# Decay sums of the SSM mixer with constant triangles as one-pass weights

## The reference

```
dt  = softplus(dt_raw + dt_bias);  a = -exp(a_log)
acum = cumsum(dt * a) over the tokens of a chunk of 128
seg[t, s] = acum[t] - acum[s]                # sum of dt*a over s < r <= t
decay = exp(where(t >= s, seg, -inf))
w = (c . b) * decay * dt ;  y = w @ x        # per head
y += c . state * exp(acum)                   # second chunk sees the first through the state
...
blocks = concat(chunks[:-1], chunks[1:]) + pos_emb   # compressed keys and values
kc = silu(blocks @ w1) @ w2
```

## Time and profile before

| | us |
|---|---|
| median of 3 runs | 870.97 (870.74 to 872.29) |
| the profiled execution | 869.12 |
| its span in the trace | 867.3 |
| PE busy | 848.3 (98%) |
| DVE busy | 602.0 (69%) |
| ACT busy | 472.5 (54%) |
| POOL busy | 63.2 (7%) |

### The profile page before, as it was taken

The page is one execution under the profiler, slowest core; times in us unless marked ns, Lnnn a source line. Parts: engine busy times, 40 slices in busy tenths (PEclk is TensorE's granted clock), DMA queues, the critical chain, the costliest instruction groups (busy, mean ns, idle before and its releaser), DMA issues.

```text
span 867.3 us, 15125 instructions
## 1 busy us (share of the span) xinstructions
PE 848.3 (98%) x5994; PEld 777.9 (90%) x5994; DVE 602.0 (69%) x805; ACT 472.5 (54%) x680; POOL 63.2 (7%) x64
## 2 busy tenths in 40 slices
PE   6999999999999999999999999999999999999997
PEld 6999999999998999899999999888887888888885
DVE  5538986537877578687776777787664686666665
ACT  5457773348665444485564555556574554444442
POOL 0025920000000232000000000000000000000000
PEclk9999999999999999999999999999999999999999
DMA  9643452333433445564555455453324365444431
GB/s 349 221 152 135 158 195 97 104 141 113 169 122 122 167 157 202 202 207 172 195 179 205 155 188 195 146 182 125 132 97 171 121 219 216 182 184 185 183 139 48
DMA packets 22169, 143.83 MB, mean 166 GB/s; under 512 B 2929, under 2 KB 3189, under 8 KB 5729
## 3 DMA queue, kind: packets, MB, share of 16 engines
q1 hardware_dynamic: 20304, 138.30, 44.4%
q0 software_dynamic: 1808, 4.73, 1.6%
HBM read 141.96 MB, written 1.84 MB: 166 GB/s over the span
## 4 chain that ended last, share of the span: by engine, by line
PE 91%; DVE 3%; ACT 3%; issue 1%; DMA 1%; SPq 0%; DVEq 0%; ACTq 0%
PE pj L467 15%; PE pj L470 12%; PE pj L469 12%; PE pa L891 7%; PE pa L892 7%; PE pa L893 7%; PE pj L1106 5%; PE pj L472 2%; PE pj L471 2%; PE pj L1108 2%; PE pa L506 2%; PE po L1106 2%; PE pj L570 1%; ACT w_hi L1152 1%; PE pj L576 1%
## 5 line engine op out<-in xcount | busy, mean ns | idle before, releaser
L1638 DVE TENSOR_TENSOR w_lo<-w_raw,w_hi 128x2048 fp32r<-128x2048 f32 x127 | 293.3, 2319 | 49.3 <-ACT w_hi L1152 49.1
L467 PE MATMUL pj<-a_hl,w_hi 128*128 128x256 f32 x944 | 269.6, 286 | 0.3 <-issue 0.3
L469 PE MATMUL pj<-a_hl,w_hi 128*128 128x256 f32 x944 | 267.0, 283 | 0.0
L470 PE MATMUL pj<-a_hl,w_lo 128*128 128x256 f32 x944 | 267.0, 283 | 0.0
L1152 ACT ACTIVATE w_hi<-w_raw 128x2048 fp32r<-128x2048 f32 x127 | 242.1, 1908 | 40.5 <-PE pa L893 22.1
L467 PEld LDWEIGHTS pj<-a_hl,w_hi 128*128 128x128 f32 x944 | 181.0, 192 | 3.4 <-issue 2.9
L469 PEld LDWEIGHTS pj<-a_hl,w_hi 128*128 128x128 f32 x944 | 181.0, 192 | 0.3
L470 PEld LDWEIGHTS pj<-a_hl,w_lo 128*128 128x128 f32 x944 | 181.0, 192 | 0.0
L891 PE MATMUL pa<-w_hi,a_hl 128*128 128x512 f32 x280 | 109.4, 391 | 0.0
L892 PE MATMUL pa<-w_lo,a_hl 128*128 128x512 f32 x280 | 109.2, 390 | 0.0
L893 PE MATMUL pa<-w_hi,a_hl 128*128 128x512 f32 x280 | 108.9, 389 | 0.0
(11 more groups left out here) (273 smaller groups left out, 1218.2 us busy)
## 6 DMA issues: line engine op xcount, KB each, us to landing
w_raw<-stream SPq DMA_DIRECT2D x127, 1024.0 KB, 4.8
area<-gains POOLq DMA_DIRECT2D x4, 512.0 KB, 4.2
cst<-consts SPq DMA_DIRECT2D x1, 1093.0 KB, 13.3
x_tok<-x_in SPq DMA_DIRECT2D x2, 512.0 KB, 4.6
w_raw<-stream SPq DMA_DIRECT2D x4, 256.0 KB, 6.7
area<-cmpw POOLq DMA_DIRECT2D x1, 1024.0 KB, 6.0
out<-x_tok SPq DMA_DIRECT2D x4, 256.0 KB, 2.0
t_wide<-t_rows POOLq DMA_DIRECT2D x1, 768.0 KB, 10.8
```

The lines of the kernel that those rows point to most:

```text
L467: pe.matmul(out_, a[0], a[1], start=first, stop=False)
L469: pe.matmul(out_, wh, al, start=False, stop=False)
L470: return pe.matmul(out_, wl, ah, start=False, stop=last)
L1638: dve.tensor_tensor(w_lo[:, slot, :], w_raw[:, slot, :], w_hi[:, slot, :].bitcast(F32), ALU.subtract)\
```

## The change

1. `seg(g)` has the constants as stationary operand and the heads' values as moving one. The operands are fp32r: `ones` and `gt` are copied once into the free chunk 20 of `a_hi` (on POOL, at the start), and dt*a is kept as a pair, high part and rest, in `dta_hl`. `gate_decay(g)` now forms `le` times dt*a for 2 chunks of the sequence and 4 heads, once for the high part and once for the rest, into free chunks of `a_hi` and `a_lo` (8 to 11 for even groups, 12 to 15 for odd). Eight products of 512 columns take the place of the twelve float32 ones.
2. The layout of `E` is by kind of block, then head: S holds two blocks (1024 columns), T one (512), and `decay` and `ssm_w` follow.
3. `gate_decay(0)` moves from between the conv blocks to behind the masked scores `cb`.
4. The four `ckp` operations move from there to behind `ssm_w(3)`.
5. `dta` takes two operations instead of one, and two more make its pair.

```
--- before.py
+++ after.py
@@ -215,7 +215,7 @@
         xbc = V(36, 16, T)
         xc = [V(52, 2, T), V(54, 2, T)]
         xs_tok, xdt = V(0, 2, D), V(8, 2, D)
-        gdt, E = V(16, 2, 4, P), V(20, 4, 384)
+        E = V(20, 3, 4, P)
         cmp_w1 = V(26, 2, 16, 64)
         nq, cb = V(34, 4, T), V(38, 4, 384)
         kk, cm, vv = V(52, 2, T), V(54, 2, T), V(56, 2, T)
@@ -248,8 +248,10 @@
         rt, rcol, eps_t, warm = small(2), small(2), small(1), small(1)
         xsum, ysum, ybias, yrt, yr = small(2), small(4), small(2), small(2), small(2)
         dgr = sb("dgr", [P, 2, P])
+        dta_hl = sb("dta_hl", [P, 2, 4, 2, 4], F32R)
+        ones_gt_r = a_hi[:, 20, :]
         small40 = small(2, 40)
-        dtx, dt_, dta = small(2, 16), small(2, 16), small(2, 16)
+        dtx, dt_, dta = small(2, 16), small(2, 16), small(4, 2, 4)
         dt_e, ea = small(2, 16), small(16)
         gate = small(2, 24)
         ssy, ry = small(2, 4), small(2, 4)
@@ -318,6 +320,11 @@
 
             return po[:, 0:T] if n % 2 else pa[:, 3, 0:T]
 
+        def decays(g, part):
+
+            c = 8 + (g % 2) * 4
+            return (a_hi, a_lo)[part][:, c:c + 4, :]
+
         def await_value(eng, name):
 
             b, n = BANK[name]
@@ -384,6 +391,9 @@
         @block.gpsimd
         def _(gp):
             G = Order(gp, "pool_order")
+
+            gp.wait_ge(S("tri_loaded"), 16)
+            gp.tensor_copy(ones_gt_r, ones_gt).then_inc(S("tri_ready"), 1)
 
             def load_gain(j):
 
@@ -724,15 +734,19 @@
 
                 claim(pe, "S", f"seg{g}")
                 claim(pe, "T", f"seg{g}")
-                pe.wait_ge(S("gdt_ready"), g + 1)
-                for m in range(4):
-                    bank = (ps, pt)[m // 2][:, m % 2, :]
-                    pe.matmul(bank[:, 0:256], gdt[:, 0, m, :], le_ones, start=True, stop=True)
-                    pe.matmul(bank[:, 128:256], dta[:, 1, 4 * g + m:4 * g + m + 1].to_broadcast([P, P]), le,
-                              start=False, stop=True, skip_group_check=True)
-                    mm = pe.matmul(bank[:, 256:384], gdt[:, 1, m, :], le, start=True, stop=True)
-                    if m == 1:
-                        written(mm, "S")
+                pe.wait_ge(S("decays_ready"), 2 * g + 2)
+                pe.wait_ge(S("tri_ready"), 1)
+                ones_r, gt_r = ones_gt_r[:, 0:P], ones_gt_r[:, P:2 * P]
+                for part in range(2):
+                    pe.matmul(ps[:, 0, :], gt_r, decays(g, part)[:, 0:2, :], start=part == 0, stop=part == 1)
+                for part in range(2):
+                    pe.matmul(ps[:, 1, :], gt_r, dta_hl[:, part, g, 0, :].unsqueeze(2).to_broadcast([P, 4, P]),
+                              start=part == 0, stop=False)
+                for part in range(2):
+                    mm = pe.matmul(ps[:, 1, :], ones_r, decays(g, part)[:, 2:4, :], start=False, stop=part == 1)
+                written(mm, "S")
+                for part in range(2):
+                    mm = pe.matmul(pt[:, 0, :], gt_r, decays(g, part)[:, 2:4, :], start=part == 0, stop=part == 1)
                 written(mm, "T")
 
             def ssm_y(g):
@@ -742,10 +756,10 @@
                     pe.wait_ge(S("xdt_ready"), 2)
                 for m in range(4):
                     c = (4 * g + m) * 64
-                    pe.matmul(po[:, m * 64:(m + 1) * 64], E[:, m, 0:128], xdt[:, 0, c:c + 64], start=True, stop=True)
-                    pe.matmul(po[:, 256 + m * 64:256 + (m + 1) * 64], E[:, m, 128:256], xdt[:, 0, c:c + 64],
+                    pe.matmul(po[:, m * 64:(m + 1) * 64], E[:, 0, m, :], xdt[:, 0, c:c + 64], start=True, stop=True)
+                    pe.matmul(po[:, 256 + m * 64:256 + (m + 1) * 64], E[:, 1, m, :], xdt[:, 0, c:c + 64],
                               start=True, stop=False)
-                    mm = pe.matmul(po[:, 256 + m * 64:256 + (m + 1) * 64], E[:, m, 256:384], xdt[:, 1, c:c + 64],
+                    mm = pe.matmul(po[:, 256 + m * 64:256 + (m + 1) * 64], E[:, 2, m, :], xdt[:, 1, c:c + 64],
                                    start=False, stop=True)
                 written(mm, "O")
 
@@ -1337,9 +1351,10 @@
                                    ACT.Copy).then_inc(S("ck_ready"), 1)
 
             def decay(g):
-                for region, bank, m in (("S", ps, 0), ("T", pt, 2)):
-                    await_psum(act, region, f"seg{g}")
-                    read(act.activation(E[:, m:m + 2, :], bank[:, :, 0:384], ACT.Exp), region)
+                await_psum(act, "S", f"seg{g}")
+                read(act.activation(E[:, 0:2, :, :], ps.rearrange("p a (m t) -> p a m t", m=4), ACT.Exp), "S")
+                await_psum(act, "T", f"seg{g}")
+                read(act.activation(E[:, 2, :, :], pt[:, 0, :].rearrange("p (m t) -> p m t", m=4), ACT.Exp), "T")
 
             token_major(("vv", 0), vv)
             decay(0)
@@ -1841,9 +1856,11 @@
             tt(ws_lo, prm[:, o:o + 320], ws_hi.bitcast(F32), ALU.subtract).then_inc(S("ws_ready"), 1)
             def gate_decay(g):
 
-                tt(gdt, gt.unsqueeze(1).unsqueeze(1).to_broadcast([P, 2, 4, P]),
-                   dta[:, :, 4 * g:4 * g + 4].unsqueeze(3).to_broadcast([P, 2, 4, P]), ALU.mult)\
-                    .then_inc(S("gdt_ready"), 1)
+                for part in range(2):
+                    d = dta_hl[:, part, g, :, :].bitcast(F32).rearrange("p t (a m) -> p (t a) m", a=2)
+                    tt(decays(g, part).rearrange("p c (m t) -> p c m t", m=2),
+                       le.unsqueeze(1).unsqueeze(1).to_broadcast([P, 4, 2, P]),
+                       d.unsqueeze(3).to_broadcast([P, 4, 2, P]), ALU.mult).then_inc(S("decays_ready"), 1)
 
             narrow_out("dt", 40)
             conv_out(0)
@@ -1857,8 +1874,13 @@
             dve.wait_ge(S("ea_ready"), 1)
             V_.did(stt(dt_, dtx, 0.0, dt_e, ALU.max, ALU.add))
             V_.sync()
-            stt(dta, dt_, -1.0, ea.unsqueeze(1).to_broadcast([P, 2, 16]), ALU.mult, ALU.mult)\
-                .then_inc(S("dta_ready"), 1)
+            for tb in range(2):
+                V_.did(stt(dta[:, :, tb, :], dt_[:, tb, :].rearrange("p (g m) -> p g m", g=4), -1.0,
+                           ea.rearrange("p (g m) -> p g m", g=4), ALU.mult, ALU.mult))
+            V_.sync()
+            V_.did(dve.tensor_copy(dta_hl[:, 0], dta))
+            V_.sync()
+            V_.did(tt(dta_hl[:, 1], dta, dta_hl[:, 0].bitcast(F32), ALU.subtract))
             conv(1)
             conv_out(2)
             sb_sum(0)
@@ -1872,7 +1894,6 @@
             conv(5)
             sb_sum(1)
             conv_out(6)
-            gate_decay(0)
             conv_taps(6)
             conv_out(7)
             sb_mask(1)
@@ -1904,10 +1925,13 @@
 
                 await_read(dve, "T", "cb")
                 await_read(dve, "S", "cb")
-                for region, m in (("S", 0), ("T", 2)):
-                    await_read(dve, region, f"seg{g}")
-                    tt(E[:, m:m + 2, :], E[:, m:m + 2, :], cb[:, g, :].unsqueeze(1).to_broadcast([P, 2, 384]),
-                       ALU.mult).then_inc(S("ssm_w_ready"), 1)
+                await_read(dve, "S", f"seg{g}")
+                tt(E[:, 0:2, :, :], E[:, 0:2, :, :],
+                   cb[:, g, 0:256].rearrange("p (a t) -> p a t", a=2).unsqueeze(2).to_broadcast([P, 2, 4, P]),
+                   ALU.mult).then_inc(S("ssm_w_ready"), 1)
+                await_read(dve, "T", f"seg{g}")
+                tt(E[:, 2, :, :], E[:, 2, :, :], cb[:, g, 256:384].unsqueeze(1).to_broadcast([P, 4, P]),
+                   ALU.mult).then_inc(S("ssm_w_ready"), 1)
 
             def ssm_out(g):
 
@@ -1918,14 +1942,7 @@
                 V_.sync()
                 read(tt(y_tok[:, :, g * 256:(g + 1) * 256], two(po), xs_tok[:, :, g * 256:(g + 1) * 256], ALU.add), "O")
 
-            dve.wait_ge(S("ck_ready"), 4)
-            pos = prm_("pos").rearrange("p (v c) -> p v c", v=2)
-            for half in range(2):
-                for v in range(2):
-                    tt(ckp[:, half, v, :].rearrange("p (n c) -> p n c", c=8),
-                       ck[:, v, :, :].rearrange("p g t -> p (g t)").rearrange("p (n c) -> p n c", c=8),
-                       pos[:, v, half * 8:half * 8 + 8].unsqueeze(1).to_broadcast([P, 32, 8]), ALU.add)\
-                        .then_inc(S("ckp_ready"), 1)
+            gate_decay(0)
             ahead(("vv", 0))
             ssm_w(0)
             gate_decay(1)
@@ -1940,6 +1957,14 @@
             ahead(("z", 0))
             ssm_out(2)
             ssm_w(3)
+            dve.wait_ge(S("ck_ready"), 4)
+            pos = prm_("pos").rearrange("p (v c) -> p v c", v=2)
+            for half in range(2):
+                for v in range(2):
+                    tt(ckp[:, half, v, :].rearrange("p (n c) -> p n c", c=8),
+                       ck[:, v, :, :].rearrange("p g t -> p (g t)").rearrange("p (n c) -> p n c", c=8),
```

(2 more changed lines are left out.)

## The result

The changed kernel has a median of 863.61 us (861.35 to 864.36, 5 runs) against 870.89 (869.35 to 872.29, 5 runs): ratio 0.993, 95% interval 0.9911 to 0.9948. Two later comparisons, each with 11 runs of the kernel before beside it, gave 0.9932 (0.9915 to 0.9949) and 0.9933 (0.9919 to 0.9947). The profiled execution has 863.37 us after 869.12, 5.75 less. Predicted were 864.5 and a gain of 6.5.

The account below looks back on a forecast made before the run. PE was taken as the bound (busy 98% of the span). Products gain 6.74 us, less a 0.2 wait, is 6.5: 862.6 for the profiled execution, 864.5 for the median; 8-in-10 range 862.9 to 867.0.

Parts of the forecast that it names:

- What bounds: Whole kernel, window 127.4 to 182 us: PE sets the time, so microseconds taken from its program come off the end.
- The products: seg(0) to seg(3): eight one-pass products take 1.81 us; gain 1.70 in group 0, 1.68 in each other, together 6.74.
- Rivals B, C and D: Pace per seg product: B four passes, 0.86 us (chance 0.03); C stalled, 0.43 (0.04); D faster, 0.13 (0.02).
- The wait of group 0: Ahead of seg(0): PE waits 0.2 us for DVE's gate_decay(0), ready at 127.6; far ends no wait and 2.6.
- my sign of being right: Ahead of seg(0) in the new trace: a PE gap of 0 to 0.3 us, released by DVE.
- rival A: Ahead of seg(0): first group's parts late by 1 to 2.6 us, gain only 4.9, time 866.1; chance 0.23.
- The advance of DVE: DVE reaches the place behind the masked scores earlier by net 0.25 to 1.0 us, taken as 0.7.
- 0.55 us later for what follows, and it runs on: DVE at 67 us: three added tiny dt*a operations delay it about 0.55 us, carried through ACT and POOL until 115.
- it is reached 0.8 to 1.57 us earlier: DVE's place behind the masked scores comes 0.8 to 1.57 us earlier with gate_decay(0) gone from 103.66, before the dt*a delay.
- POOL is helped: Conv blocks: POOL's L409 took 1.50 us beside gate_decay(0), 0.70 later; reason for taking DVE's advance on the upper side.
- What is hidden: Second gate_decay operations, weighted decays (some 3 us slack), moved ckp and POOL's copy cost PE nothing.
- The sum: Whole kernel: 6.74 - 0.2 = 6.5 us gain, predicted median 864.5 us; forecast's chance 0.68.

Follow-up runs that it names:

- high_in_gap: Changed kernel with the high-part operation of gate_decay(0) ahead of sb_lo(1), in DVE's idle gap: median 862.6 us (6 runs); timed again, 864.26.
- all_repeated: Changed kernel with all eight products of a seg reading the moving operand that repeats one value over 128 columns: 863.61 us.
- float32_form: Changed kernel with plain float32 operands, four products of 512 columns per group and no pair: 870.23 us (10 runs), ratio 1.0 to the kernel before.
- products_alone: Changed kernel with gate_decay(0) and the four ckp operations both at their old places: 866.27 us (10 runs), ratio 0.9953 to the kernel before.
- ckp_old_place: Changed kernel with the four ckp operations back behind the score masks, ahead of gate_decay(0): 865.83 us, one execution.
- pair_in_gap: Changed kernel with the two operations that make the dt*a pair moved from 68 us to DVE's gap ahead of sb_lo(1): 863.81 us.
- decay0_old_place: Changed kernel with gate_decay(0) back between conv blocks 6 and 7, ckp staying behind ssm_w(3): 865.72 us.
- after_again: The changed kernel run once more, unchanged: median 863.52 us (6 runs) against 869.14 for the kernel before; profiled execution 864.12.
- changed_2: The changed kernel, unchanged, timed again beside the second timing of the version with the high part in DVE's gap: 863.76 us.
- both_in_gap: Changed kernel with both operations of gate_decay(0) ahead of sb_lo(1), in DVE's gap: 862.66 us, one execution.
- high_only: Changed kernel without the low part: one gate_decay operation and four products per seg, dropping the rest of dt*a: 859.04 us.

## Why the prediction was right, point by point

- **What bounds.** Right. What PE's own products gained, less the wait, came off the end: 6.03 us less between two points of PE's program, 5.7 less span, nothing given back after 175 us.
- **The products.** Predicted 1.81 us per seg. Measured 1.82 where PE comes to it from a one-pass unit without a pause (`high_in_gap`), 1.90 in groups 1 to 3, where the 0.08 step from float32 now stands ahead of the products, so the gain there is 3.49 + 0.08 - 1.90 = 1.67 against 1.68. In group 0 it is 3.43 + 0.08 - 1.90 = 1.61 against 1.70, since the first pair after a pause is 0.07 slower. The repeated operand on the moving side costs nothing, it is even the faster one (`all_repeated`). That the passes and not the form give the gain is shown by `float32_form` (6.4 us against 0.3). Rivals B, C and D would have had 0.86, 0.43 and 0.13 us per product; the trace has 0.215 to 0.235. The Trainium skill's 131 ns for 512 columns in a stream ("TensorE: Matmul & The Clock Gate", Back-to-back issue gap) isn't seen in any of these kernels; the lowest spacing is 215 ns.
- **The wait of group 0.** The term that was mis-sized: 0.2 predicted, 0.67 measured. It falls between my sign of being right (0 to 0.3) and that of rival A (over 1). Its parts: DVE's advance was 0.48, not 0.7, and 0.25 of the 0.67 lies between the end of DVE's second operation (128.25) and PE's first product (128.50), which I had put at nothing. The weight load isn't this 0.25, as it starts only 0.03 ahead of the product. Ahead of it the trace has two semaphore records of PE's queue (L737 at 128.3, L738 at 128.4). Where unit `vv` waited for its split (`products_alone`), no such record stands in between, and the product came 0.10 behind DVE's end. So the rest, 0.15, goes with the waits that stand behind each other at the start of `seg`; no run changed their order. The wait is real and lost in full: 1.34 us more work ahead of it gave 1.34 more wait (`ckp_old_place`), and 1.14 less gave none (`high_in_gap`).
- **The advance of DVE.** The step "0.55 us later for what follows, and it runs on" held from 68 to 102 us in the changed kernel (0.51). That was luck in part, since with the pair taken away DVE came 0.3 us later, not earlier (`pair_in_gap`). The step "it is reached 0.8 to 1.57 us earlier", less 0.55, gave 0.48 and not 0.7, as DVE now met POOL where it hadn't: its mask took 1.02 with POOL's L425 beside it. I had raised the advance to 0.7 because POOL is helped, and that was half of it: DVE itself is held up the same way, and the 0.5 that I would have taken otherwise was the better value. The rule of the Trainium skill ("SBUF — State Buffer", Who interferes with whom), that whichever starts first holds the other back for its whole length, agrees with these rows (2.91 against 0.97 for the same POOL instruction).
- **What is hidden.** Right: no wait of `ssm_y` appeared (`ssm_w(1)` was done at 143.4 and PE asked at 146.40, the 3 us of slack as forecast), and the second operations of `gate_decay`, `ckp` and the copy on POOL (0.39 us at 13.32 us) cost nothing.
- **Why both moves belong to the change.** With neither, unit `vv` waits 2.1 us for its split (`products_alone`), with that of `ckp` alone it does too (`decay0_old_place`), and with that of `gate_decay(0)` alone `seg(0)` waits 2.0 us (`ckp_old_place`). Only both together bring the wait down to 0.67. With neither, the products give 1.3 us less in PE's stretches, and 3.2 for 5.6 in the medians. I had not priced this, as it wasn't needed for the sum.
- **The sum.** 4 segs 1.61 + 3 x 1.68 = 6.65, less 0.67: 5.98, and 6.03 was read off PE. The first medians differ by 7.28, the later ones by 5.6; the profiled executions by 5.75. So the gain of 6.5 was 0.5 too high by the traces. That 864.5 came within 0.9 of the measured 863.61 is luck in part: it was counted down from 870.97, the median of three runs, and the later comparisons have the kernel before at 869.1 to 869.5, from which the same gain gives 862.6 to 863.0.

## What to carry to other kernels

Where TensorE is the bound, count passes of columns, not instructions: a float32 product of 512 columns cost four of them here (0.86 us after 0.215 to 0.235), and with a constant that is exact in the short format on one side, splitting the other side into high part and rest makes it two. Before moving the preparation of an operand behind other work, look for a gap of the preparing engine in front of a known wait; one of 1.67 us took the 1.2 us operation for nothing. Add to the ready time what passes between the producer's end and the first product: 0.25 us here at the start of `seg(0)`, and 0.10 at that of unit `vv`. And where VectorE and GpSimd alternate, don't carry a saved half microsecond through the chain: their overlaps decide anew.

## What the runs showed of the hardware that I hadn't expected

TensorE's granted clock falls in some executions, at one place above all. Windows over 190 to 200 us, of the changed kernel's first profile and of `high_in_gap` (busy PE, PEld, DVE, ACT, POOL, then the clock):

```profile
190.00:200.00 10.00, 10.00 (x92) 9.19 (x91) 6.47 (x12) 6.84 (x16) 1.71 (x2) 1.00 0.39 125
```

```profile
190.00:200.00 10.00, 10.00 (x68) 9.18 (x67) 5.76 (x12) 6.30 (x17) 1.72 (x2) 0.68 0.40 131
```

and from the timeline of PE in the second:

```profile
191.78 3.00 PE L807 MATMUL pa<-tiny,area 64*128 64x16 f32 x32
```

Here it falls during the compressed keys' scores, products of 64 rows and 16 columns (3.00 us instead of 2.48 in the changed kernel), and the following unit's products stand 0.21 apart instead of 0.12, the lower of the two levels, until 200.4. PE was busy without a pause from 130 us to this fall. From the compressed keys' first products to the first down product it is then 157.4 us instead of 154.5 (in `high_in_gap_2` and `products_alone` too). In `after_again`, `changed_2`, `both_in_gap`, `ckp_old_place`, `float32_form` and `high_only` a shorter fall, which in all but `float32_form` begins in the unit behind these scores, makes it 155.9. In `decay0_old_place` the clock fell inside unit `vv`, behind its wait of 2.1 us, while `products_alone` had the same wait and kept its clock there. The window of 123.5 to 131 us, in this order:

```profile
123.50:131.00 7.50, 7.40 (x49) 7.43 (x50) 6.83 (x6) 3.68 (x5) 0.00 (x0) 0.77 0.74 280
```

```profile
123.50:131.00 7.50, 7.50 (x58) 7.19 (x57) 7.50 (x9) 5.58 (x8) 0.00 (x0) 1.00 0.80 282
```

Taken over all timed runs, those with a mean granted clock of 0.998 or 0.999 lie at 868.6 for the kernel before (17 runs of three comparisons), 863.3 for the changed one (9) and 861.9 for `high_in_gap` (4): 5.3 and 1.4 us apart. At 0.997 the last two lie at 863.9 (7) and 863.2 (3). But `high_in_gap` had 5 of its 12 runs at 0.995 (865.2 on the mean) and the changed kernel none of 16. Whether the absent wait makes the fall more likely or this is chance, these runs don't settle: `products_alone`, which does wait, had none of 10 above 0.997. No experiment was made on it.
